# Two transformer blocks in one program: GpSimd makes the low part of every third weight chunk in the second block's four input projections

## The reference

```python
h = _rmsnorm(x, norm1_g[l])
p = jnp.einsum('bsd,de->bse', h, w_in[l])            # 2048 x 4096: u, v, g_lru, x_lru
z_gm  = p[..., :2 * GM_WIDTH]
g_lru = p[..., 2 * GM_WIDTH:2 * GM_WIDTH + LRU_WIDTH]
x_lru = p[..., 2 * GM_WIDTH + LRU_WIDTH:]
y_gm  = _spatial_gating(jax.nn.gelu(z_gm), ...)      # v is layer-normed, mixed over tokens, times u
xr    = _causal_dwconv(x_lru, ...)
y_lru = _rg_lru(xr, ...) * jax.nn.gelu(g_lru)        # gates, exponentials, a scan over tokens
x = x + jnp.einsum('bse,ed->bsd', [norm(y_gm), norm(y_lru)], w_out[l])
```

## Time and profile before

| | us |
|---|---|
| median of 3 runs | 2366.3 (2365.81, 2366.3, 2376.13) |
| profiled execution, its own time | 2369.71 |
| its span | 2367.9 |
| granted TensorE clock, mean over the span | 0.987 |
| TensorE busy | 2277.9 (96%) |
| DVE busy | 1290.1 (54%) |
| ACT busy | 1041.4 (44%) |
| GpSimd busy | 268.2 (11%) |

### The profile page before, as it was taken

How to read it: one execution, slowest core, us unless ns; L and a number is a source line. 1 busy time by engine, 2 the same in 40 slices (tenths; PEclk the granted TensorE clock), 3 DMA queues, 4 the chain that set the end, 5 groups by cost and what they waited for, 6 DMA issues and landing times.

```text
span 2367.9 us, 30042 instructions
## 1 busy us (share of the span) xinstructions
PE 2277.9 (96%) x11859; PEld 1833.1 (77%) x11859; DVE 1290.1 (54%) x2038; ACT 1041.4 (44%) x1602; POOL 268.2 (11%) x326
## 2 busy tenths in 40 slices
PE   5889999999999999999999998999999999999998
PEld 2467777877777866678887886888888888888887
DVE  2444533332323264455776777667765777567764
ACT  2232333332322155445554466555543555445553
POOL 1000100000001022100011424111100111001111
PEclk9989999999999999999999999999999999999999
DMA  9864434345655465734566544565656555655553
GB/s 367 298 239 163 147 127 137 117 142 169 217 184 178 160 237 178 264 107 137 184 195 206 179 151 147 178 194 184 191 192 195 186 182 186 197 187 187 189 192 116
DMA packets 322427, 437.14 MB, mean 185 GB/s; under 512 B 13848, under 2 KB 220112, under 8 KB 321264
## 3 DMA queue, kind: packets, MB, share of 16 engines
q1 hardware_dynamic: 316800, 413.19, 53.0%
q0 software_dynamic: 3392, 16.90, 1.9%
q10 hardware_dynamic: 2096, 5.15, 0.7%
HBM read 428.89 MB, written 6.29 MB: 184 GB/s over the span
## 4 chain that ended last, share of the span: by engine, by line
PE 88%; DVE 4%; DMA 3%; ACT 3%; issue 1%; POOL 1%; SPq 0%; ACTq 0%; POOLq 0%
PE ps L1326 24%; PE ps L1327 12%; PE ps L1301 9%; PE ps L1303 9%; PE ps L1302 9%; PE ps L1321 5%; PE ps L1322 5%; PE ps L1323 5%; PE ps L1281 3%; DMA RAW<-in_w_in_dram 1%; PE ps L1375 1%; ACT SPL L1532 1%; DVE SPL L1775 1%; PE ps L1392 1%; DMA RAW<-in_ada_w_dram 1%
## 5 line engine op out<-in xcount | busy, mean ns | idle before, releaser
L1775 DVE TENSOR_TENSOR SPL<-RAW,SPL 128x1024 fp32r<-128x1024 f32 x592 | 752.3, 1273 | 627.3 <-ACT SPL L1532 624.6
L1326 PE MATMUL ps<-HS,SPL 128*128 128x512 f32 x2688 | 954.7, 400 | 12.0 <-DVE SPL L1775 9.1
L1532 ACT ACTIVATE SPL<-RAW 128x1024 fp32r<-128x1024 f32 x592 | 622.3, 1055 | 496.2 <-PE ps L1303 174.8
L1327 PE MATMUL ps<-HS,SPL 128*128 128x256 f32 x2688 | 754.1, 281 | 0.0
L1326 PEld LDWEIGHTS ps<-HS,SPL 128*128 128x128 f32 x2688 | 506.1, 188 | 136.5 <-DVE SPL L1775 7.1
L1327 PEld LDWEIGHTS ps<-HS,SPL 128*128 128x128 f32 x2688 | 509.0, 189 | 2.0 <-issue 1.7
L1301 PE MATMUL ps<-SPL,HS 128*128 128x512 f32 x960 | 398.8, 415 | 20.5 <-ACT XT L1574 6.2
L1303 PE MATMUL ps<-SPL,HS 128*128 128x512 f32 x960 | 379.6, 395 | 0.0
L1302 PE MATMUL ps<-SPL,HS 128*128 128x512 f32 x960 | 379.2, 395 | 0.0
L1301 PEld LDWEIGHTS ps<-SPL,HS 128*128 128x128 f32 x960 | 183.7, 191 | 83.9 <-issue 24.8
L1302 PEld LDWEIGHTS ps<-SPL,HS 128*128 128x128 f32 x960 | 183.8, 191 | 42.1 <-issue 6.0
(11 more groups left out here) (281 smaller groups left out, 1687.4 us busy)
## 6 DMA issues: line engine op xcount, KB each, us to landing
RAW<-in_w_in_dram SPq DMA_DIRECT2D x208, 512.0 KB, 5.7
RAW<-in_ada_w_dram SPq DMA_DIRECT2D x192, 512.0 KB, 4.9
RAW<-in_ffn_w_up_dram SPq DMA_DIRECT2D x192, 512.0 KB, 3.5
RAW<-in_w_out_dram SPq DMA_DIRECT2D x96, 512.0 KB, 4.4
RAW<-in_ffn_w_down_dram SPq DMA_DIRECT2D x96, 512.0 KB, 3.9
x_spill<-XT POOLq DMA_DIRECT2D x2, 2048.0 KB, 14.7
XT<-x_spill POOLq DMA_DIRECT2D x1, 4096.0 KB, 15.4
MM<-in_x_dram ACTq DMA_DIRECT2D x2, 1024.0 KB, 11.3
```

What stands on the lines that cost most here:

```text
L1326: mm(PS[b][:, :], wr, hh, start=k == 0, stop=False, skip_group_check=True)
L1327: m = mm(PS[b][:, 256:512], wl, hh[:, 0:256], start=False, stop=k == KT - 1, skip_group_check=True)
L1532: act(SPL[:, (n - 1) % NSPL, 0, :], raw_of(i), ACT.Copy).then_inc(s_hi, 1)
L1775: tt(w[:, 1, :], raw_of(s["i"]), w[:, 0, :].bitcast(F32), ALU.subtract).then_inc(s_lo, 1)
```

## The change

The splits of those chunks of stage `in2` whose number leaves 1 when divided by 3 (400, 403, ..., 463: 22 of 64) have their low part made by GpSimd in place of DVE, by the same subtraction on the same operands. GpSimd's splits count up a semaphore of their own, and what waited for the one semaphore of low parts (the load of chunk i + 8, TensorE's products) waits for that of the engine which made the low part. In exchange for the new semaphore the two of the Fourier matrix's loads, one for each layer, become one that counts on. The list of steps, its order and everything on ACT and TensorE stay.

```diff
-        s_tab, s_dft = [...], [sem(f"dft{l}_in") for l in range(2)]
+        s_tab, s_dft = [...], sem("dft_in")
-        s_hi, s_lo, s_chunk, s_part = sem("split_hi"), sem("split_lo"), ...
+        s_hi, s_lo, s_lop, s_chunk, s_part = sem("split_hi"), sem("split_lo_dve"), sem("split_lo_pool"), ...
...
-                    last = [(s_lo, split_no[i])]
+                    last = [low_done[i]]
...
-                    put("split", i=i, last=last)
+                    on_pool = queue[i].group.stage == "in2" and i % 3 == 1
+                    low_done[i] = (s_lop, tick("lop")) if on_pool else (s_lo, tick("lo"))
+                    put("split", i=i, last=last, on_pool=on_pool)
...
-                    e.wait_ge(s_lo, split_no[i])            # tensor
+                    e.wait_ge(*low_done[i])
...
-                    for sm, v in new(*s["ready"], (s_dft[s["l"]], 16)):
+                    for sm, v in new(*s["ready"], (s_dft, 16 * (s["l"] + 1))):
...
-                if kind == "split":                         # vector
+                if kind == "split" and not s["on_pool"]:
...
+                if kind == "split" and s["on_pool"]:        # gpsimd
+                    w = SPL[:, (n - 1) % NSPL, :, :]
+                    e.wait_ge(s_hi, n)
+                    tt(w[:, 1, :], raw_of(s["i"]), w[:, 0, :].bitcast(F32), ALU.subtract).then_inc(s_lop, 1)
```

More of the change, by code:

```diff
@@ L176, in two_block_program @@
         s_raw = [sem(f"raw{i}_in") for i in range(NRAW)]
-        s_tab, s_dft = [sem(f"rope{l}_in") for l in range(2)], [sem(f"dft{l}_in") for l in range(2)]
+        s_tab, s_dft = [sem(f"rope{l}_in") for l in range(2)], sem("dft_in")
         s_ap = [sem(f"pool_matrix{l}_in") for l in range(2)]
@@ L182, in two_block_program @@
         s_memset, s_colT, s_col, s_c = sem("memsets"), sem("rows_turned"), sem("columns"), sem("silu_c")
-        s_hi, s_lo, s_chunk, s_part = sem("split_hi"), sem("split_lo"), sem("chunk_multiplied"), sem("part_multiplied")
+        s_hi, s_lo, s_lop, s_chunk, s_part = sem("split_hi"), sem("split_lo_dve"), sem("split_lo_pool"), sem("chunk_multiplied"), sem("part_multiplied")
         s_sqx, s_turn, s_xt = sem("x_squares"), sem("x_turned"), sem("x_columns")
@@ L232, in two_block_program @@
         at = {"loaded": 0, "taken": 0, "split": 0, "used": 0, "pos": 0, "ahead": AHEAD}
-        split_no, chunk_split = {}, {}
+        split_no, chunk_split, low_done = {}, {}, {}
         hi, low = [], []
@@ L2190, in gpsimd @@
                 kind, n = s["kind"], s["n"]
-                if kind == "spill":
+                if kind == "split" and s["on_pool"]:
+                    w = SPL[:, (n - 1) % NSPL, :, :]
+                    e.wait_ge(s_hi, n)
+                    tt(w[:, 1, :], raw_of(s["i"]), w[:, 0, :].bitcast(F32), ALU.subtract).then_inc(s_lop, 1)
+                elif kind == "spill":
                     for sm, v in new((s_xt, KT), *s["last"]):
@@ L2231, in gpsimd @@
                         e.wait_ge(sm, v)
-                    e.dma_start(lay[l].CS, I["k_dft"].rearrange("(t p) c -> p t c", p=128)).then_inc(s_dft[l], 16)
+                    e.dma_start(lay[l].CS, I["k_dft"].rearrange("(t p) c -> p t c", p=128)).then_inc(s_dft, 16)
                 elif kind == "n0":
```

## The result

The changed kernel is slower by 0.6%. The first comparison gave a median of 2385.14 us (4 executions, 2383.45 to 2385.77) beside 2367.01 us for the kernel before (4 executions), ratio 1.0061 [1.0044, 1.0078]. A second one, with more executions, gave 2383.15 (5) beside 2368.41 (11), ratio 1.006 [1.0047, 1.0072]: 14.7 us. The ratio is formed over all the executions of a comparison and not from the two medians; 14.7 us is the figure that I go by, and its ratio's interval is worth 11 to 17 us.

What follows compares the result with a forecast made beforehand. TensorE, 96% busy, was taken as the bound, its stage losing time at four short places. 2.8 + 2 + 0.7 + 4 = 9.5 us gave 2379 us for the profiled execution, median 2376; range 2368.5 to 2385.

Steps and rivals of the forecast that it cites:

- the seven named parts: Splits 403, 421, 424, 451, 457, 460 and 463, at the places where the prediction expected moved parts to cost time.
- A: Norms at 1250 us: split 403 delays the power, lengthening TensorE's wait and perhaps low-clock time; 2.8 us (1.4 to 4.2).
- B: Norm of v, 1300 to 1318 us: split 421 holds back L2078, split 424 comes late; 2 us (0 to 3.3).
- C: Last convolution at 1397 us: split 451 on GpSimd frees it or holds it back; 0.7 us (-0.7 to 1.4).
- D: Scans and g_lru, 1423 to 1467 us: splits 457, 460, 463 and `y2` come late; 4 us (1.9 to 5.5).
- everything covered: Rival: DVE wins the meetings, only split 403's delay and splits 457 and 460 cost; 3.3 us or less, 2369; chance 0.17.
- held back everywhere: Rival: each of the 22 parts costs its 1.2 us, spare time does not hold; about 18 us, 2384; chance 0.17.
- relief wins: Rival: faster, as splits 421, 451, 460 and 463 leave DVE's chains; at most 5 us, 2361; chance 0.06.
- Nothing behind gives it back: After the stage: with TensorE 96% busy, little later idle time could absorb the stage's delay.
- the high part of 463 some 4 us later against the stage's start: Sign in g_lru that would show the forecast: ACT's high part of chunk 463 some 4 us later.

Runs made afterwards that it cites:

- the quiet fifteen: Changed kernel with chunks 403, 421, 424, 451, 457, 460 and 463 split by DVE again: 2371.91 us beside 2371.2 for the kernel before, ratio 1.0000.
- the seven: Kernel before with only the low parts of chunks 403, 421, 424, 451, 457, 460, 463 on GpSimd: 2382.38 us beside 2371.2, ratio 1.0046.
- only 403: Kernel before with only chunk 403's low part on GpSimd: 2375.18 us beside 2371.2, ratio 1.0015.
- the last three: Kernel before with only the low parts of chunks 457, 460 and 463 on GpSimd: 2374.76 us beside 2368.41, ratio 1.0029.
- where DVE is late: Kernel before with only the low parts of chunks 423, 458 and 459 on GpSimd: 2376.28 us beside 2370.34, ratio 1.0034.
- the halves: Changed kernel, but GpSimd makes only columns 512 to 1023 of each moved part and DVE the rest: 2378.19 us beside 2370.46 for before, ratio 1.0029.
- behind the power: Changed kernel with GpSimd issuing split 403 behind the power of both norms: 2378.22 us beside 2368.41 for the kernel before, ratio 1.0042.
- behind the diagonals: Changed kernel with split 403 behind the power of both norms and held until DVE's diagonals are made: 2377.57 us beside 2370.46 for before, ratio 1.003.
- 460 behind y2: Changed kernel with split 460 moved behind the fourth `y2` in GpSimd's queue: 2378.28 us beside 2368.41 for the kernel before, ratio 1.0041.
- the Fourier semaphores merged: Kernel before with only the Fourier matrix's two semaphores made one, every split on DVE: 2370.91 us beside 2371.2, ratio 0.9999.
- y rows one by one: Kernel before, no part on GpSimd; planner takes the first eight tiles' `y0`, `y1`, `y2` one at a time: 2369.78 us beside 2370.46, ratio 0.9998.

## Why the prediction was right, and where its sum fell short

*Direction, mechanism and places.* Right. The moved part takes 2.4 us; the cost lies in the seven named parts (the quiet fifteen: ratio 1.0000; the seven: 11.2 us) and arises at A, B, C and D. A was taken alone ("only 403") and D was ("the last three"); B and C are read from their steps in the table and from the timelines, and no run has them alone. Of the rivals, "everything covered" (3.3 us) falls with the 14.7 us, "held back everywhere" with the quiet fifteen, and "relief wins" with the result itself and with "where DVE is late"; the halves, slower too, tested it only in part. One choice went the less likely way: staying within 0.5% had a chance of 0.62, slower than that 0.37, and 0.61% [0.44, 0.78] is slower.

*The sum.* 9.5 us forecast; 13.4 in the profiled execution, inside the forecast's bounds of 2.6 to 14.4, and 14.7 by the medians, 0.3 us over them. The measured cost is 1.4 to 1.55 times the sum. By terms:

| term | forecast (bounds) | measured |
|---|---|---|
| A | 2.8 (1.4 to 4.2) | 4.2 |
| B | 2 (0 to 3.3) | 2.4 |
| C | 0.7 (-0.7 to 1.4) | 0.9 |
| chunks 450 to 456 | none | 0.3 |
| D, to chunk 464 | 4 (1.9 to 5.5) | 3.7 |
| behind chunk 464 | none | 1.9 |

*A was mis-sized, and by another way than I wrote.* I had the power wait for split 403 in GpSimd's queue, or `bare_lo` and the means for the part itself, 1.4 to 2.5 us. What happened is the second kind, but through DVE's part of 404, which I had not in the sum, and it lost 3.4 us. That A came out just at its upper bound of 4.2 is chance. "Only 403", "behind the power" and "behind the diagonals" (4.2, 2.9 and 0.0 us at chunk 402) show that the meeting makes the cost. The clock's share, which I had put at up to 1.7 us, was 0.8: in the changed kernel two pieces stand at 1.2 GHz near the norms, 3.4 us from 1248.2 and 6.8 us from 1255.1, where before has one of 3.4 us, but the first of them only fills time in which TensorE would have waited.

*B and C* came by the ways forecast: L2080 held back by split 421, split 424 held back and waited for, the convolution held back by split 451. Of L2080's 2.1 us only 1.3 reached TensorE, and at the low part of 423 instead of at `v_mix`.

*D to chunk 464* came as forecast, with 1.4 us up to chunk 460 (forecast 1.9 for this part), the `y2` of the fourth tile 3.5 us late counted from chunk 456 (forecast 4), the high part of 463 2.2 us (about 3), its low part 3.7 us (3.6), and TensorE's longest wait 6.3 us (7.1). The clock had no part in it: I had read 6.8 us at the lower clock beside the wait of 5.2 us and left out the 3.4 us in 1430 to 1440, and the changed kernel has the same 10.2 us. "460 behind y2" puts 0.7 us of the 3.7 to that queue order, less than I had given the chain. The sign "the high part of 463 some 4 us later against the stage's start" did not fit my own sum, by which A, B, C and 3 us come to 8.5; it came 10.05 us later.

*"Nothing behind gives it back"* was right, but more was lost: 1.5 us at chunks 471 to 473, in a piece of 3.4 us at 1.2 GHz from 1497.4 us. TensorE's waits for `y2` there (2.8 us, three times, longest 1.4) are the same in the quiet fifteen, which has no such piece. It appears in most kernels that are late at 464, and not in "460 behind y2"; but "only 403" has it too, with its waits in g_lru as before, and so has "the Fourier semaphores merged", with no part on GpSimd. So these 1.5 us are not shown to be a cost of the change. What decides them is open.

*Rows and rules.* L2080 and the diagonals were held for 2.1 us each by a part issued 0.07 and 0.04 us ahead of them. By the Trainium skill (SBUF — State Buffer, Who interferes with whom) whoever issues first keeps the shared ports; at these two places the trace agrees. At the low part of 404 it doesn't, by the starts that the profile gives (below). The 2.6 cycles per element of the Trainium skill (GPSIMD Engine Reference, Elementwise — side-by-side cycle accounting), which made the part an estimated 2.2 us, is under the measured 2.40 us.

*What hit the range's edge.* The range was 2368.5 to 2385 around a median of 2366.3 us from three executions. The first comparison's median of 2385.14 lies 0.14 us above its top; with its ratio of 1.0061 on the 2366.3 it would be 2380.7, inside. My own bounds for the median were 2369 to 2381. Longer series of the kernel before gave 2368.41 to 2371.2 us, so the start was some 2 to 5 us low, and part of the miss in the absolute time is that start. The difference, 14.7 us, is free of it.

## What to carry to other kernels

Moving an operation to GpSimd has two prices: its own longer time, and that of every DVE operation which it meets. Both are nothing while the ring of buffers has room (here fifteen parts of 2.4 us for 0.0 us), and both are paid, in full or in part, where DVE's queue leads straight to a waiting TensorE (one part for 4 us). So look in the trace, for each single moved instruction, for what DVE will have under way in those microseconds and who waits for it; the busy shares don't tell. A wait that is lengthened can also bring more time at the lower clock, but count only what lies behind the wait: at the norms 6.8 us more at 1.2 GHz went with 0.8 us of cost, and in g_lru the longer wait brought none.

## What the runs showed that I had not expected

*The first to start did not always win.* DVE's low part of chunk 404 had been under way for 1.14 us, of the 1.23 that it needs, when GpSimd's part of 403 began at 1250.60; it ended at 1254.09, 1.09 us after GpSimd's end at 1253.00. It is no chance: it took 4.63, 4.62 and 4.59 us in the changed kernel, the seven and only 403. In the quiet fifteen, with the same DMA issues of GpSimd beside it but no part of 403, the same instruction took 1.23 us:

```profile
1249.50 1.23 DVE L1777 TENSOR_TENSOR SPL<-RAW,SPL 128x1024 fp32r<-128x1024 f32 x1
```

The 1.09 us behind GpSimd's end are what a DVE part also needs that starts well inside one of GpSimd's. The same kernel has such a pair 11 us earlier, with an end 1.08 us behind GpSimd's:

```profile
1238.02 2.50 POOL L2197 TENSOR_TENSOR SPL<-RAW,SPL 128x1024 fp32r<-128x1024 f32 x1 [1.96 <-ACT SPL L1534]
...
1239.33 2.27 DVE L1777 TENSOR_TENSOR SPL<-RAW,SPL 128x1024 fp32r<-128x1024 f32 x1 [1.08 <-ACT SPL L1534]
```

So it looks as if the part of 404 had made next to no headway in its first 1.14 us, as it would if GpSimd's instruction held it from before the start that the profile gives. No run here tests that, and it stays open.

*A copy is held too.* In "403 behind the diagonals" DVE's copy of two columns, 0.16 us in the quiet fifteen, took 2.38 us beside that part. Nobody waited for it.

*A gain can vanish behind the place where it is made.* With the y rows one by one, TensorE's longest wait in the stage fell from 5.2 to 1.8 us and chunk 460 came 3.8 us sooner; eleven chunks later nothing was left of it.
